# A three-part transformer on one core: the mLSTM convolution three units earlier, and a step between the two halves of the forget gate's logarithm

## What is computed

```python
def hybrid_layer(x, norm_w, w_in, conv_w, conv_b, gate_bias, ret_norm_w, mlstm_norm_w, w_out):
    h = rmsnorm(x, norm_w)
    proj = jnp.matmul(h, w_in)
    (aq, ak, av, ag, bq, bk, bv, bg, cq, ck, cv, co, cg, ci, cf) = jnp.split(proj, cuts, axis=-1)
    ...
    qk = jax.nn.silu(causal_dwconv(jnp.concatenate([cq, ck], axis=-1), conv_w, conv_b))
    ...
    yc = mlstm(cq_c, ck_c, cv, i_pre, f_pre)          # per head; chunks of 128
    yc = yc * split_heads(jax.nn.sigmoid(co), C_HEADS)
    yc = head_norm(yc, mlstm_norm_w) * jax.nn.silu(cg)
    ...
    return x + jnp.matmul(y, w_out)

def mlstm(q, k, v, i_pre, f_pre):
    ...
    bc = jnp.cumsum(jax.nn.log_sigmoid(f_pre)...)     # the forget gate's logarithm
    d_log = jnp.where(causal, bt[..., :, None] - bt[..., None, :] + it[..., None, :], -jnp.inf)
    m_t = jnp.maximum(inter_log, jnp.max(d_log, axis=-1))
    sc = jnp.einsum('bhtd,bhsd->bhts', qt, kt) * jnp.exp(d_log - m_t[..., None])
```

## Time and profile before

| | us |
|---|---|
| median of 3 runs | 2398.74 (2397.21 to 2401.32) |
| the profiled execution, its own time | 2403.04 |
| its span in the profile | 2401.3 |
| PE busy | 2298.4 (96%) |
| DVE busy | 1593.6 (66%) |
| ACT busy | 886.9 (37%) |
| POOL busy | 239.4 (10%) |

### The profile page before, as it was taken

How to read it: one execution, slowest core, us unless ns; L and a number is a source line. 1 busy time by engine, 2 the same in 40 slices (tenths; PEclk the granted TensorE clock), 3 DMA queues, 4 the chain that set the end, 5 groups by cost and what they waited for, 6 DMA issues and landing times.

```text
span 2401.3 us, 33023 instructions
## 1 busy us (share of the span) xinstructions
PE 2298.4 (96%) x13198; PEld 1960.8 (82%) x13198; DVE 1593.6 (66%) x2898; ACT 886.9 (37%) x1507; POOL 239.4 (10%) x321
## 2 busy tenths in 40 slices
PE   6988988999999999999999999999999999998998
PEld 6877878988888777777888888888888888798998
DVE  5787787787877547875589866653333356876665
ACT  4344344422222344533332222232222234654443
POOL 1002000100102200012111111200000030021001
PEclk9998899999999999999999999999999999998999
DMA  7444443565654321122256665423222233254553
GB/s 263 159 138 146 153 159 122 178 210 181 214 175 149 114 68 63 59 88 92 80 195 234 211 210 203 149 82 103 97 94 91 97 112 106 97 160 143 184 185 121
DMA packets 97657, 341.31 MB, mean 142 GB/s; under 512 B 11312, under 2 KB 13488, under 8 KB 97120
## 3 DMA queue, kind: packets, MB, share of 16 engines
q1 hardware_dynamic: 74144, 254.46, 31.5%
q0 software_dynamic: 23360, 84.74, 11.0%
HBM read 338.11 MB, written 2.48 MB: 142 GB/s over the span
## 4 chain that ended last, share of the span: by engine, by line
PE 77%; DVE 13%; issue 5%; ACT 4%; POOL 1%; DMA 0%; POOLq 0%; DVEq 0%; ACTq 0%
PE PS L573 76%; DVE WL L1244 3%; ACT WH L942 2%; PE PS L893 1%; DVE HL L1253 1%; DVE NT L1253 1%; DVE JK L1254 1%; ACT P L943 1%; DVE AR L1254 1%; POOL ACC L1835 1%; DVE PJB L1253 1%; DVE CV L1253 1%; DVE P L1248 0%; POOL SS L1835 0%; DVE ST L1257 0%
## 5 line engine op out<-in xcount | busy, mean ns | idle before, releaser
L942 ACT ACTIVATE WH<-RAW 128x1024 fp32r<-128x1024 f32 (+3 forms) x498 | 511.6, 1028 | 993.4 <-PE PS L573 993.2
L573 PE MATMUL PS<-HH,WH 128*128 128x512 f32 (+1 forms) x2240 | 777.5, 347 | 7.8 <-DVE HL L1253 4.1
L573 PE MATMUL PS<-HL,WH 128*128 128x512 f32 (+1 forms) x2240 | 768.0, 343 | 0.0
L573 PE MATMUL PS<-HH,WL 128*128 128x512 f32 (+1 forms) x2240 | 768.0, 343 | 0.0
L1244 DVE TENSOR_TENSOR WL<-RAW,WH 128x1024 fp32r<-128x1024 f32 (+3 forms) x498 | 590.4, 1186 | 141.2 <-ACT WH L942 140.2
L573 PEld LDWEIGHTS PS<-HH,WH 128*128 128x128 f32 x2240 | 426.9, 191 | 67.5 <-DVE HL L1253 6.3
L573 PEld LDWEIGHTS PS<-HH,WL 128*128 128x128 f32 x2240 | 426.8, 191 | 52.7
L573 PEld LDWEIGHTS PS<-HL,WH 128*128 128x128 f32 x2240 | 427.0, 191 | 51.5
L573 PE MATMUL PS<-GH,WH 128*128 128x512 f32 (+1 forms) x776 | 271.1, 349 | 0.3 <-DVE WL L1244 0.3
L573 PE MATMUL PS<-GH,WL 128*128 128x512 f32 (+1 forms) x776 | 270.1, 348 | 0.0
L573 PE MATMUL PS<-GL,WH 128*128 128x512 f32 (+1 forms) x776 | 270.1, 348 | 0.0
(11 more groups left out here) (220 smaller groups left out, 2813.2 us busy)
## 6 DMA issues: line engine op xcount, KB each, us to landing
RAW<-in_wst SPq DMA_DIRECT2D x436, 512.0 KB, 3.5
AR<-in_w_adaT POOLq DMA_DIRECT2D x144, 512.0 KB, 3.8
RAW<-in_wst SPq DMA_DIRECT2D x48, 384.0 KB, 3.0
BM<-rpb_rows POOLq DMA_DIRECT2D x48, 64.0 KB, 3.0
CB<-in_cc POOLq DMA_DIRECT2D x2, 1024.0 KB, 10.3
RAW<-in_wst SPq DMA_DIRECT2D x8, 256.0 KB, 2.7
RAW<-in_wst SPq DMA_DIRECT2D x4, 396.0 KB, 3.0
rpb_rows<-in_rpb POOLq DMA_DIRECT2D x2, 697.5 KB, 11.6
```

Of the source, the lines that this page charges most:

```text
L573: return e.matmul(o, l, r, start=start, stop=stop)
L942: return e.activation(o, i, f, bias=bias, scale=scale)
```

## The change

It writes the list of steps and four generators anew. In both layers of block 1 three M steps are set beside the three `vcg` units, so that three of the four convolution steps are issued there, and the fourth beside the first `pj` unit. In layer 1 the two E steps of this part are set at other places. The logarithm gets a `yield` between its first half (DVE `g1`, ACT `g2` and `g3`) and `g4`, so that `g4` comes one M step later; ACT, PE and POOL get a `yield` each to match. Two M steps fewer stand beside later gate units, so that the sum of M steps is 33 in place of 32 for each layer.

```diff
-        order += mix(D=7, E=2) if l else mix(D=7)
+        order += mix(D=4, E=1) + mix(D=3, M=3, E=1) if l else mix(D=4) + mix(D=3, M=3)
         order += ["Q"] if l else ["K"]
...
         feat("w_in", l, 1792, 2, "silu", "H1", l, 256, 10)
-        order += mix(D=2, M=2) + heads(1, 1)
+        order += mix(D=2, M=1) + heads(1, 1)
         feat("w_in", l, 4096, 2, "silu", "H1", l, 256, 18)
-        order += mix(D=2, M=2) + ["M", "M"] + heads(2, 1)
+        order += mix(D=2, M=1) + ["M", "M"] + heads(2, 1)
...
         def mlstm():
             P = PS[3]
             for l in range(DEPTH):
-                for _ in range(5):
+                for _ in range(6):
                     yield
                 q.wait_ge(*vm.at("g4", l))
...
                 af(T1, T2, ACT.Ln, bias=ONE[:, 0:1]).then_inc(*am.inc("g3", l))
+                yield
                 yield
                 yield
...
                 stt(T1, F_, -1.0, F_, ALU.mult, ALU.max).then_inc(*vm.inc("g1", l))
+                yield
                 q.wait_ge(*am.at("g3", l))
...
             for l in range(DEPTH):
-                for _ in range(27):
+                for _ in range(28):
                     yield
                 q.wait_ge(*vm.at("var", l))
```

## The result

| | before | after |
|---|---|---|
| median, us (6 runs each) | 2399.51 (2396.50 to 2401.47) | 2409.68 (2406.11 to 2411.94) |
| the profiled execution's own time, us | 2403.04 | 2408.28 |

The ratio is 1.0044, 95% interval 1.0031 to 1.0057: slower by 10.6 us (7.4 to 13.7; the two medians differ by 10.2). The forecast was 6.6 us slower, 2405.3, range 2398 to 2411. The measured time lies in this range, but above the forecast's own 2403 to 2408.

What follows compares the result with a forecast made beforehand. PE, busy 96% of 2401.3 us, was taken as the bound, losing time to idling and lowered clock. Terms +2.9 + 4.5 - 1.7 + 0.9 gave +6.6 us on the 2398.74 median: 2405.3, range 2398 to 2411.

Steps and rivals of the forecast that it cites:

- Layer 0's idle time: From mLSTM's values to the first gate unit, layer 0: PE idle 8.7 us against 5.8, so +2.9 us.
- p1 to p3: First three of the four units after mLSTM's values' units; in layer 0 PE waits 1.3, 1.1, 1.2 us for WL.
- The table load with 1.30 us to the next operation: On ACT before the tanh AR in layer 0: 1.30 us, from the trace; the skill's 2.66 us would make +4.3.
- Layer 1's idle time: Same stretch in layer 1: PE idle 10.9 us against 6.4, from three WL waits and one for MI; +4.5 us.
- Clock: Lowered PE clock in both stretches: layer 0 unchanged, layer 1 loses 5.1 us against 6.8, so -1.7 us.
- Later steps: After the first gate units, mLSTM two steps ahead in the retention stretch: +0.9 us, bounds -2 and +4.
- The 3.2 us are gone, hidden by p3 and p4: Layer 0: PE's 3.2 us wait for the logarithm vanishes because it is issued a step ahead, covered by two units' work.
- Faster: PE doesn't stop at MI: 2393.0 us, chance 1 in 10; needs layer 0's AR tanh to start at 50.1.
- Much slower: Layer 1's second diagonal also stalls PE, or the waits after the values' units lower the clock: 2408.7 to 2410, 1 in 10.
- Even: Waits as counted, but less clock loss: 2401.8 with layer 0's loss gone, 2396.7 with both gone; chance 2 in 10.

## Why the prediction was right in sign, and where its sum was wrong

- **Layer 0's idle time** (forecast 8.7 against 5.8, +2.9): 8.5, +2.7. p1 to p3 waited 1.29, 0.93 and 0.91 (forecast 1.3, 1.1, 1.2), MI 5.41 (5.1). The table load with 1.30 us to the next operation held: AR starts at 55.51, 1.30 after 54.21.
- **Layer 1's idle time** (10.9 against 6.4, +4.5): 8.1, +1.7; mis-sized by 2.8. p1 3.6 (3.3), MI 1.8 (2.0), but p2 none (1.1) and p3 2.7 (4.5). With layer 1 changed alone p3 waits 3.88, nearer the walk. In the changed kernel PE works on p1 at the lower clock level after its stall, and so comes later to p2 and p3; the row below, of the windows view from 239.2 to 244.9 us, has 0.50. But p3's start is set by the chain of DVE and ACT, as walked. From p1's start to p3's it is 11.33 us in the changed kernel, at a mean clock of 0.74, and 11.34 with layer 1 changed alone, at 0.81 (231.78 to 243.12). A lower clock there turns idle time into busy time and costs nothing, while the prediction added the two.

```profile
239.20:244.90 5.70, 5.68 (x26) 5.70 (x27) 5.03 (x11) 2.69 (x8) 1.97 (x3) 0.50 0.39 136
```

PE's timeline in the changed kernel, p1 and p3:

```profile
239.22 0.55 PE L573 MATMUL PS<-H1H,WH 128*128 128x256 f32 x1 [3.58 <-DVE WL L1245]
...
250.55 0.36 PE L573 MATMUL PS<-H1H,WH 128*128 128x256 f32 x1 [2.72 <-DVE WL L1245]
```

- **Clock** (-1.7): 0.88 by 43.7 us is 5.2 against 6.8, -1.6; in layer 0 nothing, as forecast.
- **Later steps** (+0.9): 2.3 and 3.8 us, +6.1. This is the step that failed. It counted the known waits of the retention stretch and never walked DVE's queue to the gate units behind attention's values, where a low part had no slack. The waits that it did count moved little: the second diagonal's in layer 0 fell from 1.9 to 1.3. The bound given, +4, was too small as well, by idle time and by the measured runs: set back, these steps return 9.6 us, some 2 of them at MI; added alone, they cost 7.9. By length, the profile pair shows 3.8.
- **The reason for the gain.** "The 3.2 us are gone, hidden by p3 and p4" came true, but the split of the logarithm wasn't what they hung on: CB's product and its tanh were, and they stall MI next. Moved away, they free the wait with the logarithm undivided (0.4 us), and with the split kept but CB's product ahead of `g4` the wait stays at 3.3.
- **Rivals.** *Faster* failed at the point named: AR's tanh came at 55.5, not 50.1. *Much slower*, given 1 in 10, had the size, 2408.7 to 2410, but not the mechanism: layer 1's second diagonal waits 0.3 us, and layer 0's p1 to p3 run at full clock. Its upper end doesn't follow from its terms either, which give 2408.9 and 2408.7 apart and 2412.3 together. *Even* failed too: layer 0's clock loss stayed and the idle time grew.

The two mis-sized terms partly cancel: 2.7 + 1.7 - 1.6 + 6.1 is 8.9 against 6.6 forecast and 10.6 measured. By length the two walked stretches grew by 3.3 us where 5.7 were forecast, and the rest by 3.8 where 0.9 was. So it is in part luck that the time fell into the range: the walked stretches were forecast 2.4 us too dear and the rest 2.9 too cheap.

## What to carry to other kernels

A stream that is moved forward is ahead until its last step. Walk the waiting engine's queue through every stretch that it crosses, and look first for operands that arrive just in time: there a rearranged microsecond can count in full. In this case 3.1 us of delay at such an operand became 2.8 us of waiting. Before a wait is put down to the operation that releases it, read what stands ahead of that operation in its queue; here an unrelated product of 2.3 us, with its tanh, had been taken for the logarithm.

## What the hardware showed that was not expected

Three of DVE's `scalar_tensor_tensor` over 256 columns take 1.52 us, and 2.75 us while POOL adds tiles of the same size (rows above; in the changed kernel 2.73 at 243.78). The Trainium skill (GPSIMD Engine Reference, Key points) says that POOL shares its SBUF interfaces with VectorE and contends with instructions of two SBUF inputs; the trace agrees, at 1.8 times the duration. The run with the squares behind o4 bears it out. There the fourth step's three operations, at 238.15, take 1.53 us again, and the squares' adds (4.29 us on POOL from 262.65) fall on retention's rotation instead. DVE's timeline:

```profile
264.25 0.41 DVE L1246 TENSOR_TENSOR RT<-PS,CS 128x256 f32<-128x256 f32 x1
264.58 0.89 DVE L1246 TENSOR_TENSOR PJB<-PJB,CS 128x256 f32<-128x256 f32 x1
...
272.54 0.42 DVE L1246 TENSOR_TENSOR PJB<-PJB,CS 128x256 f32<-128x256 f32 x1
```

With both inputs in SBUF the product takes 0.89 us beside POOL and 0.42 without it; the one with an input from PSUM keeps its 0.41 beside POOL.

Stretches of the same order differ by execution: the 762 us from 1177 to 1939 us of before took 3.7 us less in the changed kernel's profile, and 758.2 to 762.9 over all fourteen profiles. No run here tells why.
